# Two units of the expert modulation moved ahead of the conv branch's sums of squares, and one weight load moved behind the gate chunk's loads

## The chip, the cores and the metric

The kernel runs on one core of a Trainium2 chip. The metric is the device time of one execution in microseconds (us). Engine names are those of the profile: PE is TensorE (PEld its weight loads), DVE is VectorE, ACT is ScalarE, POOL is GpSimd, SP is SyncE, which issues the loads of all large weights.

## The reference

A trunk of two layers works on 256 tokens of width 1024. Each layer is modulated by six vectors that come from the conditioning vector `c`, and has a mixer (conv heads beside attention heads) and a mixture of 16 experts:

```python
for l in range(DEPTH):
    mod = (c_act @ w_ada[l] + b_ada[l])[:, None, :]
    shift1, scale1, gate1, shift2, scale2, gate2 = jnp.split(mod, 6, axis=-1)
    h = rmsnorm(x, norm1_g[l]) * (1.0 + scale1) + shift1
    u = h @ w_in[l]
    u_b, u_c, u_h, u_q, u_k, u_v = jnp.split(u, split_at, axis=-1)
    y_conv = short_conv_mixer(u_b, u_c, u_h, conv_w[l])
    ...
    y_att = moba_attention(q, k, v).transpose(0, 2, 1, 3).reshape(B, S, aw)
    y_mix = jnp.concatenate(
        [rmsnorm(y_conv, conv_out_g[l]), rmsnorm(y_att, attn_out_g[l])], axis=-1)
    x = x + gate1 * (y_mix @ w_out[l])
    h2 = rmsnorm(x, norm2_g[l]) * (1.0 + scale2) + shift2
    x = x + gate2 * hier_moe(h2, ...)
```

## The kernel before

All code is written by hand for each engine: an engine runs its instructions in the order in which the program lists them, and semaphores tie the engines together.

**Units and the ring.** All weights come to SBUF in units of 1 MB, into a ring of ten slots (`raw`, `RAW = 10`). The list `stream` gives the order in which SP loads them. Before a load SP waits until the unit that held the slot, ten places earlier in `stream`, is used up (`wait_free`). SP works in order, so a wait for one slot holds back all loads behind it. The kinds of unit that matter here:

- `("w", l, u)`, u = 0 to 11: the input projection `w_in`, called w0 to w11 below. The units of u = 10 and 11 hold the columns of the values `v`; u = 12 to 15 (w12 to w15) hold `w_out`. ACT copies each half of such a unit to `whi` (L500), DVE subtracts to get the low part `wlo` (L790), and PE multiplies both in three passes. A w unit is used up when DVE has made its second half (`lo_done`).
- `("a", chunk, k)`: unit k of a modulation chunk, the product of `c` with columns of `w_ada`. The chunk `G` (units G0 to G7) gives the two gates, `M` (M0 to M7) gives shift and scale of the expert sub-layer, and in layer 0 `A` (A0 to A7) gives those of the next layer's mixer. PE multiplies them in `ada_acc` (L1248, eight rows of the profile to a unit) straight from `raw`, all into PSUM bank 6, and a unit is used up when PE has done so (`ada_used`).
- `("g", ...)` and `("d", ...)`: gate, up and down weights of the experts, multiplied by PE from `raw` (L1559 and L1585).

**The mixer on PE, in order** (line numbers of the profile): the input projection of q, k and two conv parts (`in_half`, L1347 and L1354); units G0 to G3; the transposes of q and k (L1383); G4 to G7; scores of the first heads (L1397); the projection of the third conv part (halves 16 to 19, L1347) with the transposes of probabilities between (L1405); more scores; the projection of the values (halves 20 to 23, L1354); four matmuls with a matrix of ones that sum the squares of the conv output over channels (L1449); the products with the values (L1415 to L1417); M0 to M7 (L1248); the output projection (`out_half`, L1462).

**Around the sums of squares.** DVE makes the conv output (L1003 to L1007), ACT squares it (L640) and signals `csq_ready`, and PE waits for that signal ahead of L1449. ACT then takes a root (L644), and DVE scales the conv output and splits it (to L1021, `ymc_ready`), for which `out_half` waits.

**Around the units G.** DVE waits for the last unit G to add a bias (`gate_row`, L886) and then takes the maxima of the scores (L970, L975), ACT the exponentials (L590). Behind these ACT and DVE split w11 (halves 22 and 23), which the projection of the values needs.

Of the kernel before, what the change touches and what calls it, by code (L numbers as in the profile page):

```python
# [30 lines left out]
def trunk(nc, x, c, positions, norm1_g, norm2_g, w_ada, b_ada, w_in, conv_w, q_norm_g, k_norm_g,  # L31
          conv_out_g, attn_out_g, w_out, w_rg, b_rg, w_re, b_re, w_gate, w_up, w_down, out):
    _, S, D = x.shape
    L = norm1_g.shape[0]
    CW = conv_out_g.shape[1]
    AW = attn_out_g.shape[1]
    HD = q_norm_g.shape[1]
    H = AW // HD
    NE, _, F = w_gate.shape[1:]
    NG = w_rg.shape[2]  # L40
    EG = NE // NG
# [21 lines left out]
    with ExitStack() as ctx:  # L63
# [218 lines left out]
        stream = [("a", 0, k) for k in range(4)] + [("w", 0, 0), ("w", 0, 1)]  # L282
        stream += [("a", 1, 0), ("a", 1, 1), ("w", 0, 2), ("a", 1, 2), ("a", 1, 3)]
        for l in range(L):
            stream += [("w", l, u) for u in range(3 if l == 0 else 2, 12)]
            stream += [("a", chunk_of[("G", l)], k) for k in range(KD)]
            stream += [("w", l, u) for u in range(12, 16)]
            stream += [("a", chunk_of[("M", l)], k) for k in range(KD)]
            if l + 1 < L:
                stream += [("a", chunk_of[("A", l + 1)], k) for k in range(KD)]  # L290
            for p in range(NP + 1):
                if p < NP:
                    stream += [("g", l, (2 * p + i, h)) for h in range(2) for i in range(2)]
                if p > 0:
                    stream += [("d", l, 2 * (p - 1) + i) for i in range(2)]
            if l + 1 < L:
                stream += [("w", l + 1, u) for u in range(2)]
            stream.append(("x", l, 0))
# [935 lines left out]
        def _(pe):  # L1234
            def ada_acc(kind, l, ks):

                q = chunk_of[(kind, l)]
                if ks[0] == 0 and q > 0:
                    pe.wait_ge(mod_evac, steps_before[q])
                    before_q = sum(1 for name, _ in chunks[:q] if name == "G")  # L1240
                    if before_q:
                        pe.wait_ge(gate_row_ready, before_q)
                for k in ks:
                    unit = ("a", q, k)
                    pe.wait_ge(raw_full[ring_slot[unit]], landed[unit])
                    for i in range(4):
                        row = 2 * k + i // 2 if q < 2 else k
                        ins = pe.matmul(ps[32 * i:32 * i + 32, 6, :], c_rep[:, row, :],  # L1248
                                        raw[:, ring_slot[unit], i * 512:(i + 1) * 512],
                                        start=(k == 0), stop=(k == chunk_units[q] - 1), skip_group_check=True)  # L1250
                    ins.then_inc(ada_used, 1)
# [51 lines left out]
            def wait_half(l, i):  # L1303
                n = HALVES * l + i
                pe.wait_ge(lo_done, n + 1)
                return whi[:, slot(n), :], wlo[:, slot(n), :]
# [24 lines left out]
            for l in range(L):  # L1331
# [6 lines left out]
                def in_half(n, bank, k0, by_channel):  # L1338
                    w = wait_half(l, n)
                    for kk in range(2):  # L1340
                        k = k0 + kk
                        if l == 0 and n == 4 and kk == 1:
                            ada_acc("A1", 0, range(2, 4))
                        if by_channel:
                            for j in range(KC):
                                for p, (pa, pw) in enumerate(PASSES):
                                    ins = pe.matmul(ps[:, bank + j // 2, (j % 2) * S:(j % 2 + 1) * S],  # L1347
                                                    w[pw][:, kk * 512 + j * P:kk * 512 + (j + 1) * P],
                                                    acts[pa][:, k, :], start=(k == 0 and p == 0 and j % 2 == 0),
                                                    stop=(k == KD - 1 and p == 2), skip_group_check=True)  # L1350
                        else:
                            for t in range(T):
                                for p, (pa, pw) in enumerate(PASSES):
                                    ins = pe.matmul(ps[:, bank + t, :], acts[pa][:, k, t * P:(t + 1) * P],  # L1354
                                                    w[pw][:, kk * 512:(kk + 1) * 512],
                                                    start=(k == 0 and p == 0), stop=(k == KD - 1 and p == 2))
                    ins.then_inc(unit_used, 1)
# [43 lines left out]
                def probs_T(u):  # L1401
                    pe.wait_ge(exp_done, 4 * l + u + 1)
                    for h, bank, p in heads(u):
                        for q in range(3):
                            ins = pe.transpose(ps[:, bank, q * P:(q + 1) * P], p[:, q * P:(q + 1) * P],  # L1405
                                               ident[:, :])
                    ins.then_inc(pT_done, 1)

                def values(a):
                    for h in range(4 * a, 4 * a + 4):  # L1410
                        p = work[:, h // 4, h % 4, :]
                        vs = slice(h * HD, (h + 1) * HD)
                        c0 = 2 * HD * (h % 4)
                        y0, y1 = slice(c0, c0 + HD), slice(c0 + HD, c0 + 2 * HD)
                        pe.matmul(ps[:, a, y0], p[:, 0:P], v_sb[:, 0, vs], start=True, stop=True)  # L1415
                        pe.matmul(ps[:, a, y1], p[:, P:2 * P], v_sb[:, 0, vs], start=True, stop=False)
                        ins = pe.matmul(ps[:, a, y1], p[:, 2 * P:3 * P], v_sb[:, 1, vs], start=False, stop=True)  # L1417
                    ins.then_inc(pv_done, 1)
# [25 lines left out]
                probs_T(2)  # L1444
                probs_T(3)
                in_half(23, 4, 6, False)
                pe.wait_ge(csq_ready, l + 1)
                for j in range(KC):
                    ins = pe.matmul(ps[:, 7, S:2 * S], ones[:, :], cb[:, j, :], start=(j == 0), stop=(j == KC - 1))  # L1449
# [2 lines left out]
                pe.wait_ge(proj_evac, 5 * (l + 1))  # L1452
                values(0)
                values(1)
                ada_acc("M", l, range(0, 8))

                def out_half(s, half, t, ns):
                    w = wait_half(l, 24 + 4 * s + half)
# [195 lines left out]
                with pe.If(pe.value_load(over_i[0:1, l:l + 1], min_val=0, max_val=1) > 0):  # L1654
# [10 lines left out]
                    for e in range(NE):  # L1665
                        loads = X_LOADS * l + 16 * 5 * e
                        for half in range(2):
                            pe.wait_ge(x_full, loads + 32 * (half + 1))
                            w = stage.rearrange("p (g k f) -> p g k f", g=2, k=4)
# [51 lines left out]
```

## Time and profile before

| | before |
|---|---|
| median of 3 runs | 581.92 us (581.85 to 581.98) |
| profiled execution | 583.74 us |
| its span, first to last instruction | 581.8 us |
| mean granted TensorE clock | 0.978 |
| PE busy | 548.2 us, 94% |
| DVE busy | 278.4 us, 48% |
| ACT busy | 224.3 us, 39% |
| memory read | 188.12 MB, 325 GB/s over the span |

The span is what the views of the trace show; 1.94 us of the profiled execution lie around it. Busy shares are means over stages with different limits.

### The profile page before, as it was taken

How to read it: one execution, taken by the hardware profiler on the slowest of the kernel's cores; microseconds unless marked ns; L12 is line 12 of the kernel's file. 1: busy time of each engine (PE TensorE's matmuls, PEld its weight loads, DVE VectorE, ACT ScalarE, POOL GpSimd, SP SyncE). 2: the span in 40 equal slices, each digit the busy share in tenths (PEclk: the TensorE clock that was granted, in tenths of full speed). 3: DMA queues.
4: the chain of work that ended last, by engine and by line, in shares of the span. 5: the costliest groups of instructions: out<-in, count | busy, mean ns of one | idle time of the engine just before them, and what ended most of it. 6: DMA issues, size and time to landing. Idle time of an engine off the chain costs nothing.

```text
span 581.8 us, 8006 instructions
## 1 busy us (share of the span) xinstructions
PE 548.2 (94%) x3222; PEld 356.2 (61%) x3222; DVE 278.4 (48%) x475; ACT 224.3 (39%) x386; POOL 17.0 (3%) x74
## 2 busy tenths in 40 slices
PE   7899989999999999999978999999996999999996
PEld 6578939868666344443357897786674744444433
DVE  3629954993481022222358489479438202222243
ACT  2527445632346222221237264554314623222121
POOL 3105000000000000000000000000000000000000
PEclk9999999999989999999979999999997999999999
DMA  8999993972999999999997743499288379999961
GB/s 303 386 386 367 402 353 144 424 309 96 425 408 412 413 414 413 414 413 411 403 387 282 277 151 126 190 402 393 74 315 335 137 296 394 413 413 413 412 269 75
DMA packets 51759, 189.79 MB, mean 326 GB/s; under 512 B 4650, under 2 KB 4730, under 8 KB 44292
## 3 DMA queue, kind: packets, MB, share of 16 engines
q1 hardware_dynamic: 50496, 185.62, 81.8%
q0 software_dynamic: 896, 2.45, 1.2%
q10 hardware_dynamic: 324, 1.13, 0.6%
q8 instruction: 29, 0.48, 0.3%
q14 instruction: 14, 0.11, 0.1%
HBM read 188.12 MB, written 1.06 MB: 325 GB/s over the span
## 4 chain that ended last, share of the span: by engine, by line
PE 69%; DVE 17%; DMA 6%; ACT 3%; issue 2%; SPq 1%; DVEq 0%; ACTq 0%
PE ps L1559 18%; PE ps L1585 9%; PE ps L1462 7%; PE ps L1539 6%; PE ps L1354 6%; PE ps L1347 6%; DVE wlo L790 5%; PE ps L1248 5%; PE ps L1601 4%; DMA raw<-in_w_ada_dram 4%; DMA raw<-in_w_down_dram 2%; DVE work L952 2%; DVE cbc L1005 1%; DVE tokmaj L947 1%; SPq L325 1%
## 5 line engine op out<-in xcount | busy, mean ns | idle before, releaser
L790 DVE TENSOR_TENSOR wlo<-raw,whi 128x1024 fp32r<-128x1024 f32 x64 | 75.6, 1220 | 35.6 <-ACT whi L500 35.4
L500 ACT ACTIVATE whi<-raw 128x1024 fp32r<-128x1024 f32 x64 | 65.4, 1057 | 36.5 <-PE ps L1347 14.3
L1559 PE MATMUL ps<-raw,qkT 128*64 128x512 f32 x256 | 58.3, 597 | 1.6 <-ACT work L740 1.6
L1585 PE MATMUL ps<-raw,work 128*64 128x512 f32 x256 | 58.5, 598 | 1.1 <-DMA raw<-in_w_down_dram 1.1
L1559 PE MATMUL ps<-raw,cbc 128*64 128x512 f32 x256 | 57.6, 594 | 0.0
L1185 DVE SCALAR_TENSOR_TENSOR work<-ps,cw,work 128x256 f32<-128x256 f32 x16 | 10.9, 683 | 95.8 <-ACT work L734 95.8
L1171 DVE TENSOR_TENSOR v_sb<-ps,gates 128x512 f32<-128x512 f32 x32 | 22.1, 692 | 69.1 <-PE ps L1585 69.1
L1347 PE MATMUL ps<-act_hi,whi 128*128 128x256 f32 x192 | 54.9, 286 | 0.0
L1347 PE MATMUL ps<-act_hi,wlo 128*128 128x256 f32 x192 | 54.3, 283 | 0.0
L1347 PE MATMUL ps<-act_lo,whi 128*128 128x256 f32 x192 | 54.3, 283 | 0.0
L1248 PE MATMUL ps<-raw,c_rep 128*32 128x512 f32 x384 | 45.6, 605 | 4.0 <-DMA raw<-in_w_ada_dram 4.0
L722 ACT ACTIVATE whi<-v_sb 128x512 fp32r<-128x512 f32 x32 | 20.2, 630 | 58.0 <-DVE v_sb L1171 58.0
L1559 PEld LDWEIGHTS ps<-raw,cbc 128*64 128x64 f32 x256 | 18.5, 137 | 34.3 <-issue 33.2
L1354 PE MATMUL ps<-whi,act_hi 128*128 128x512 f32 x96 | 38.1, 397 | 1.3 <-DVE act_lo L893 1.3
L1347 PEld LDWEIGHTS ps<-act_hi,whi 128*128 128x128 f32 x192 | 36.8, 192 | 2.5 <-issue 2.3
L1539 PEld LDWEIGHTS ps<-whi,act_hi 128*128 128x128 f32 x128 | 26.7, 209 | 18.2 <-issue 18.2
L1539 PE MATMUL ps<-whi,act_hi 128*128 128x256 f32 x128 | 37.4, 321 | 0.3 <-DVE whi L1122 0.3
L1559 PEld LDWEIGHTS ps<-raw,qkT 128*64 128x64 f32 x256 | 17.3, 137 | 33.1 <-issue 28.0
L1354 PE MATMUL ps<-wlo,act_hi 128*128 128x512 f32 x96 | 37.4, 390 | 0.0
L1354 PE MATMUL ps<-whi,act_lo 128*128 128x512 f32 x96 | 37.4, 389 | 0.0
L1585 PEld LDWEIGHTS ps<-raw,work 128*64 128x64 f32 x256 | 17.4, 136 | 32.5 <-issue 31.7
L1347 PEld LDWEIGHTS ps<-act_hi,wlo 128*128 128x128 f32 x192 | 36.8, 192 | 0.1
(239 smaller groups left out, 862.7 us busy)
## 6 DMA issues: line engine op xcount, KB each, us to landing
raw<-in_w_ada_dram SPq DMA_DIRECT2D x40, 1024.0 KB, 12.7
raw<-in_w_gate_dram SPq DMA_DIRECT2D x64, 512.0 KB, 8.3
raw<-in_w_up_dram SPq DMA_DIRECT2D x64, 512.0 KB, 9.8
raw<-in_w_down_dram SPq DMA_DIRECT2D x32, 1024.0 KB, 11.3
raw<-in_w_in_dram SPq DMA_DIRECT2D x23, 1024.0 KB, 14.3
raw<-in_w_ada_dram SPq DMA_DIRECT2D x16, 512.0 KB, 11.4
raw<-in_w_out_dram SPq DMA_DIRECT2D x8, 1024.0 KB, 7.0
gates<-gate_line POOLq DMA_DIRECT2D x2, 1024.0 KB, 5.1
```

The lines of the kernel that those rows point to most:

```text
L500: act.activation(whi[:, slot(n), :], raw[:, r, (i % 2) * 1024:(i % 2 + 1) * 1024], ACT.Copy).then_inc(hi_done, 1)
L722: act.activation(y_hi[:, cols], y_f[:, cols], ACT.Copy).then_inc(yhi_ready, 1)
L790: dve.tensor_tensor(wlo[:, slot(n), :], raw[:, ring_slot[("w", l, i // 2)], (i % 2) * 1024:(i % 2 + 1) * 1024], whi[:, slot(n), :].bitcast ...
L1171: dve.tensor_tensor(y_f[:, cols], ps[:, 2 + n, :], gates[:, 1, cols], ALU.mult).then_inc(yg_ready, 1)
L1248: ins = pe.matmul(ps[32 * i:32 * i + 32, 6, :], c_rep[:, row, :], raw[:, ring_slot[unit], i * 512:(i + 1) * 512], start=(k == 0), stop=(k ...
L1347: ins = pe.matmul(ps[:, bank + j // 2, (j % 2) * S:(j % 2 + 1) * S], w[pw][:, kk * 512 + j * P:kk * 512 + (j + 1) * P], acts[pa][:, k, :], ...
L1354: ins = pe.matmul(ps[:, bank + t, :], acts[pa][:, k, t * P:(t + 1) * P], w[pw][:, kk * 512:(kk + 1) * 512], start=(k == 0 and p == 0), sto ...
L1462: ins = pe.matmul(ps[:, 2 * t + n, :], acts[pa][:, k, t * P:(t + 1) * P], w[pw][:, n * 512:(n + 1) * 512], start=(k == 0 and p == 0), stop ...
L1539: ins = pe.matmul(ps[:, bank, j * S:(j + 1) * S], xn[part][:, t, k * P:(k + 1) * P], sel[:, t, 256 * q:256 * (q + 1)], start=(t == 0 and p ...
L1559: ins = pe.matmul(ps[i * SLOTS:(i + 1) * SLOTS, 0, :], hg[p // 2 % 2][:, k, c0:c0 + SLOTS], ws[i][:, :, kk, :], start=(k == 0), stop=(k == ...
L1585: ins = pe.matmul(ps[i * SLOTS:(i + 1) * SLOTS, 2 + n, :], hidT[:, p % 2, kk, i * SLOTS:(i + 1) * SLOTS], ws[i][:, c0:c0 + 512], start=(kk ...
L1601: ins = pe.matmul(ps[:, 4 + 2 * t + n, :], selT[:, 2 * p + t, :], ys[part][:, n * 512:(n + 1) * 512], start=(p == 0 and part == 0), stop=( ...
```

## The change

Two edits, each in both layers. In `stream`, w11 is loaded behind the eight units of G and not ahead of them. In PE's program, units M0 and M1 are multiplied ahead of the wait for `csq_ready`, and M2 to M7 stay where the whole chunk stood.

```diff
         for l in range(L):
-            stream += [("w", l, u) for u in range(3 if l == 0 else 2, 12)]
+            stream += [("w", l, u) for u in range(3 if l == 0 else 2, 11)]
             stream += [("a", chunk_of[("G", l)], k) for k in range(KD)]
-            stream += [("w", l, u) for u in range(12, 16)]
+            stream += [("w", l, u) for u in range(11, 16)]
             stream += [("a", chunk_of[("M", l)], k) for k in range(KD)]
...
                 in_half(23, 4, 6, False)
+                ada_acc("M", l, range(0, 2))
                 pe.wait_ge(csq_ready, l + 1)
                 for j in range(KC):
                     ins = pe.matmul(ps[:, 7, S:2 * S], ones[:, :], cb[:, j, :], start=(j == 0), stop=(j == KC - 1))
...
                 values(0)
                 values(1)
-                ada_acc("M", l, range(0, 8))
+                ada_acc("M", l, range(2, 8))
```

On SP, at the end of the input projection's loads in layer 0 (`in_w_in` are w units up to w11, `in_w_ada` of 128x2x1024 the units G, `in_w_out` w12 to w15, `in_w_ada` of 128x2048 the units M and A):

```order
 L325 DMA raw<-in_w_ada_dram 128x2x512 x4
-L339 DMA raw<-in_w_in_dram 128x4x512 x9
+L339 DMA raw<-in_w_in_dram 128x4x512 x8
 L334 DMA raw<-in_w_ada_dram 128x2x1024 x8
+L339 DMA raw<-in_w_in_dram 128x4x512
 L344 DMA raw<-in_w_out_dram 128x2x1024 x4
 L334 DMA raw<-in_w_ada_dram 128x2048 x16
```

One load, w11, has moved from ahead of the eight loads of G to behind them; all others keep their order. Since the ring goes round by place in the list, the units G now take the slots that were their predecessors' (G7 the slot that w8 held, where it was w9's), w11 takes the slot of w9, and from w12 on every unit has its old slot. In some of these slots the holder has changed: w13, w14 and w15 now follow G0, G1 and G2 (before: w11, G0 and G1), M0 to M4 follow G3 to G7 (before: G2 to G6), and M5 follows w11 (before: G7).

On PE, at the end of the projection of the values in layer 0 (the last two matmuls of `in_half(23)`, then the sums of squares and the first products with the values; a row of 32x512 is a matmul of a unit of M, four to a unit):

```order
 L1354 MATMUL ps<-wlo,act_hi 128x512
 L1354 MATMUL ps<-whi,act_lo 128x512
-L1449 MATMUL ps<-cbc,ones 128x256 x4
+L1248 MATMUL ps<-raw,c_rep 32x512 x8
+L1450 MATMUL ps<-cbc,ones 128x256 x4
 L1415 MATMUL ps<-v_sb,work 128x64
 L1416 MATMUL ps<-v_sb,work 128x64
```

Eight matmuls, the units M0 and M1, now stand between the projection of the values and the sums of squares; behind the products with the values 24 of the 32 matmuls of the chunk are left. The line added moves the numbers behind it up by one.

## Rows read from the trace of the kernel before

**Rows 1.** The page: busy time of PE; GB/s in 40 slices of 14.5 us.
```profile
PE 548.2 (94%) x3222; PEld 356.2 (61%) x3222; DVE 278.4 (48%) x475; ACT 224.3 (39%) x386; POOL 17.0 (3%) x74
GB/s 303 386 386 367 402 353 144 424 309 96 425 408 412 413 414 413 414 413 411 403 387 282 277 151 126 190 402 393 74 315 335 137 296 394 413 413 413 412 269 75
```

**Rows 2.** Chain of waits, layer 0's mixer: start us, us, what.
```profile
78.13 6.80 DMA raw<-in_w_ada_dram
...
115.32 1.24 DVE cbc L1007
116.58 1.06 ACT cbc L640
```

**Rows 3.** Timeline of PE, layer 0: start us, us, instructions, [idle before <-releaser].
```profile
79.55 1.92 PE L1248 MATMUL ps<-raw,c_rep 128*32 128x512 f32 x16
82.46 1.07 PE L1248 MATMUL ps<-raw,c_rep 128*32 128x512 f32 x8 [0.98 <-DMA raw<-in_w_ada_dram]
84.98 1.79 PE L1248 MATMUL ps<-raw,c_rep 128*32 128x512 f32 x8 [1.46 <-DMA raw<-in_w_ada_dram]
86.70 2.57 PE L1397 MATMUL ps<-qkT 64*128 64x128 f32 x16
89.20 0.38 PE L1347 MATMUL ps<-act_hi,whi 128*128 128x256 f32 x1
...
117.69 1.99 PE L1449 MATMUL ps<-cbc,ones 128*128 128x256 f32 x8 [1.37 <-ACT cbc L640]
...
124.92 7.07 PE L1248 MATMUL ps<-raw,c_rep 128*32 128x512 f32 x64
131.92 0.73 PE L1462 MATMUL ps<-whi,act_hi 128*128 128x512 f32 x2
```

**Rows 4.** Timeline of PE, layer 1, the same places.
```profile
362.56 2.78 PE L1248 MATMUL ps<-raw,c_rep 128*32 128x512 f32 x24
366.00 1.06 PE L1248 MATMUL ps<-raw,c_rep 128*32 128x512 f32 x8 [0.66 <-DMA raw<-in_w_ada_dram]
367.00 1.69 PE L1397 MATMUL ps<-qkT 64*128 64x128 f32 x16
368.62 0.38 PE L1347 MATMUL ps<-act_hi,whi 128*128 128x256 f32 x1
...
397.10 1.99 PE L1449 MATMUL ps<-cbc,ones 128*128 128x256 f32 x8 [1.36 <-ACT cbc L640]
```

**Rows 5.** Windows, 84 to 90 us: after busy times, granted clock, DMA share, GB/s.
```profile
84.00:85.00 1.00, 0.02 (x3) 0.02 (x4) 0.00 (x0) 0.00 (x0) 0.00 (x0) 1.00 1.01 410
85.00:86.00 1.00, 1.00 (x8) 0.14 (x8) 0.00 (x0) 0.00 (x0) 0.00 (x0) 0.59 0.52 209
87.00:88.00 1.00, 1.00 (x8) 0.92 (x7) 0.51 (x1) 0.00 (x0) 0.20 (x1) 0.50 0.00 0
89.00:90.00 1.00, 1.00 (x9) 0.81 (x7) 0.96 (x3) 0.00 (x0) 0.23 (x1) 1.00 0.01 0
```

**Rows 6.** Timeline of SP, layer 0: loads of G6, G7, w12 and w13 to w15.
```profile
70.74 0.37 SPq L334 DMA_DIRECT2D raw<-in_w_ada_dram  x1
78.13 0.37 SPq L334 DMA_DIRECT2D raw<-in_w_ada_dram  x1
80.40 0.37 SPq L344 DMA_DIRECT2D raw<-in_w_out_dram  x1
97.66 1.39 SPq L344 DMA_DIRECT2D raw<-in_w_out_dram  x3
```

**Rows 7.** DMA issues from 70 to 71 us (G6): KB each, median us to landing.
```profile
raw<-in_w_ada_dram SPq DMA_DIRECT2D x1, 1024.0 KB, 11.7
```

**Rows 8.** Timeline of ACT, layer 0: the copies of w11's two halves.
```profile
94.14 2.23 ACT L500 ACTIVATE whi<-raw 128x1024 fp32r<-128x1024 f32 x2
```

**Rows 9.** Timeline of DVE, layer 0: the conv output's low part (`ymc_ready`).
```profile
124.66 1.23 DVE L1021 TENSOR_TENSOR act_lo<-cbc,act_hi 128x1024 fp32r<-128x1024 f32 x1
```

**Rows 10.** Timeline of PE, layer 0's expert stage: its one wait for a load.
```profile
280.86 1.51 PE L1585 MATMUL ps<-raw,work 128*64 128x512 f32 x6 [1.12 <-DMA raw<-in_w_down_dram]
```

## The prediction

> **What bounds the kernel now.** I read the page first: PE is busy for 548.2 of 581.8 us [rows 1], so time is won only where PE itself waits, or runs slowly. Then the chain of waits, in order of time, for the places where it leaves PE. In layer 0's mixer it does so twice near the edits: it goes through a load that SP issued at 78.13 and that took 6.80 us to land, and through DVE and ACT at 115.32 to 117.64 [rows 2]. PE's timeline gives the size of these holes: 0.98 us ahead of unit G6 and 1.46 us ahead of G7, both for a load, and 1.37 us ahead of the sums of squares, for ACT's squares [rows 3]. In layer 1 they are 0.66 and 1.36 us [rows 4]. A third cost shows when the two layers are laid side by side. From the start of G7 to the start of the scores PE takes 1.72 us in layer 0 (84.98 to 86.70) and 1.00 us in layer 1 (366.00 to 367.00); the scores take 2.50 us (86.70 to 89.20) against 1.62 us (367.00 to 368.62) [rows 3, 4]. The windows say why: behind the stretch in which PE stood still for 2.44 us, the granted clock drops to 0.59 and 0.50 and is back at 1.00 only when the scores are over [rows 5]; 0.50 is the lower of the two levels, 1.2 GHz, and 1.00 the upper, 2.4 GHz.
>
> **The loads of G.** G7 waits for the slot of w9, so SP issues it at 78.13, when DVE has split w9; G6, in the slot of w8, goes at 70.74 [rows 6]. G6 lands 11.7 us after its issue [rows 7], at 82.4, when PE starts on it; G7 lands at 84.93 [rows 2]. So G6 was behind other loads (one unit lands each 2.5 us), and G7 behind G6. With w11 taken out ahead of them each unit G gets the issue time, the slot and the place in the queue of the unit ahead of it: G7 is issued at 70.74 and lands at 82.4, G6 lands a unit earlier, near 79.9, and w11 takes what was G7's, issue at 78.13 and landing at 84.93.
>
> PE runs a unit in 0.875 us (7.00 us from 124.92 to 131.92 for eight [rows 3]). From 79.55 it does G4, G5 and G6 until 82.18, waits some 0.3 us, and starts G7 at 82.46 where it started at 84.98: 2.52 us. With the hole down to 0.3 us I take the clock to stay up, so that G7 and the scores cost what they cost in layer 1: 1.72 − 1.00 = 0.72 and 2.50 − 1.62 = 0.88 us. Layer 0 gains 2.52 + 0.72 + 0.88 = 4.12 us here. If the clock falls all the same, 2.52.
>
> In layer 1 G7 gets an issue time one unit earlier in the same way, and the hole of 0.66 us goes; the clock was up there already.
>
> What follows must come earlier too. DVE's maxima and ACT's exponentials hang on G7 and the scores and move with them; the projection behind them uses w8 to w10, which are split by 80.4, when SP could issue w12 into w10's slot [rows 6]. The next in line is **w11**: ACT copies it right behind the exponentials, at 94.14 [rows 8], in the new order near 90.0. It lands at 84.93, 5.1 us ahead. That is the cover that makes moving it free; each us beyond it would hold ACT, with the probabilities' copies queued behind it, for which PE's next scores wait.
>
> SP has less to wait for behind w12. Today w13 waits for w11's slot until 97.66, and w14, w15 and the first six of M stand behind it [rows 6]. Now w13 takes the slot of G0, long multiplied, so w13 to w15 and M0 to M4 follow w12 as fast as SP issues and G4 to G7 are used. At 2.5 us a unit, nine units behind w11 are there by 84.93 + 9 × 2.5 = 107.4. The bus was idle in that time: 144 GB/s in the slice from 87.3 to 101.8 [rows 1].
>
> **M0 and M1 ahead of the sums of squares.** In the trace's own times PE is free at 117.69 − 1.37 = 116.32. Two units take 1.75 us, until 118.07, so the squares, ready at 117.64, wait 0.4 us, and the chunk behind the values is 1.75 us shorter. Net the hole of 1.37 us is filled, 1.36 in layer 1. By the above M0 and M1 are there before 107. What the split chunk costs extra the trace does not show: two more changes between kinds of matmul. The nearest row is G7 ahead of the scores in layer 1, 1.00 us against 0.875, so 0.1 us; bounds 0 and 0.3 per layer. I take 0.1. The 0.4 us by which the sums end later go to ACT's root and DVE's split, which ends at 125.89 [rows 9] where the output projection starts at 131.92 [rows 3]: 6.0 us of room, of which the shorter chunk eats 1.3 and the delay 0.4.
>
> **Behind the mixer.** The output projection, the routing and the experts follow PE. The loads of the A chunk and the experts wait in SP for w14, w15 and the units M and A, the last of them paced by PE's output projection, so they come earlier along with it. I count the gain of the mixer in full.
>
> **Sum.** Layer 0: 4.12 + 1.37 − 0.1 = 5.4. Layer 1: 0.66 + 1.36 − 0.1 = 1.9. Together 7.3 us. The profiled span of 581.8 us becomes 574.5; its execution of 583.74 lies 1.82 above the median, so I take the gain off the median: 581.92 − 7.3 = **574.6 us**.
>
> **Rivals.**
> *The clock falls anyway* (PE's hole ahead of G7 does not quite close, or its time in G is too thin). Layer 0 loses 0.72 + 0.88: gain 5.7, 576.2 us. For it: at the routing and between layers PE has low stretches too, and a shift of some us may lengthen or shorten them, by a like amount. Against: eight units of M in a row run at 0.875 each, as G4 and G5 do.
>
> *M0 and M1 buy nothing*, because something else holds the output projection, such as the conv branch's split or the attention norm: 581.92 − 4.12 − 0.66 = 577.1 us. Against it are the 6.0 us of room.
>
> *The expert stage is bound by its loads.* For it: 408 to 414 GB/s through layer 0's experts, without a dip [rows 1]. If the stream of loads starts no earlier, layer 0's 5.4 us come back as waits of PE: 581.92 − 1.9 = 580.0 us. Against: in that stage PE waits for a load once, 1.12 us [rows 10], and what releases the loads moves. The Trainium skill speaks for this rival: its page "DMA: Bandwidth & Descriptors", section Specifications, puts the ceiling of the path into SBUF at 435 GB/s; the row's 413 is 95% of that, so by the page loads that start late could hardly catch up.
>
> *Slower: w11 comes late.* If the loads in flight shared the bandwidth instead of landing in order of issue, w11 would land with the nine behind it, at 107.4, and ACT, due at 90.0, would stand for 17.4 us: layer 0 ends 12.0 us later than now, 581.92 − 1.9 + 12.0 = 592 us. It decides from a landing at 90.0 + 7.3 = 97.3 on. Against: G7, with w12 issued 2.27 us behind it, landed 2.5 us after G6, one unit's time. The same page, section "Queues, rings and completion order", warns that "completion is **not FIFO per issuing engine**"; by it w11 could lose its place, by the row it does not, and I go by the row.
>
> *The edits do nothing*: the holes close but what comes next was as late, 581.9.
>
> **How the numbers follow.** The full gain: 0.58, own range 573.5 to 575.7. The clock falls: 0.15. M0 and M1 buy nothing: 0.08. Loads bind the experts: 0.06. Slower by w11: 0.05. Nothing: 0.04. A larger gain, through less time at the low clock later on, 571 to 573.4: 0.04. From 572.5 to 578.5 stand the first three and part of the larger gain, 0.83. The unknown switch cost (0 to 0.6 in sum) is inside. A measurement here tells 0.2% (1.2 us) from no change: faster 0.91, same 0.04, slower 0.05.
>
> **What would show it.** In the new trace: G7 starts without a hole of more than 0.5 us in both layers; the scores of layer 0 start 3.2 us earlier (near 83.5) at a clock of 1.00; ACT's copies of w11 start right behind the exponentials with no wait for a load; w13 to w15 are issued near 81, not 97.66; the hole ahead of L1450 is gone in both layers and the output projection of layer 0 starts near 126.5, that of layer 1 7.3 us earlier than now; PE's waits for loads among the experts stay near 1 us. I am wrong if w11 holds ACT, if the clock still dips near 85, or if waits for expert weights grow by what the mixer gave.

## The result and the profile after

The changed kernel took 579.18 us (median of 8 executions, 577.28 to 581.14), the kernel before 583.04 us (8 executions, 581.85 to 587.24): a ratio of 0.9937 with a 95% interval of 0.9916 to 0.9958. It is faster by 0.4 to 0.8%, 3.7 us by the ratio and 3.9 by the medians where 7.3 were forecast, and the 579.18 us lie above the range given. The three executions on which the forecast was based were also quick ones: the median of before rose from 581.92 to 583.04 with five more.

The profiled execution took 577.56 us. The page of the changed kernel:

```profile
span 575.8 us, 8006 instructions
...
PE 548.0 (95%) x3222; PEld 356.4 (62%) x3222; DVE 278.4 (48%) x475; ACT 224.4 (39%) x386; POOL 17.0 (3%) x74
...
PEclk9899999999989999999979999999995999999999
...
GB/s 304 388 387 368 406 382 418 373 126 155 420 408 413 413 414 414 412 415 414 397 386 291 257 147 130 414 422 131 103 381 246 147 310 408 405 415 413 412 265 76
```

The seventh slice now moves 418 GB/s where it moved 144 [rows 1]: w13 to w15 and the first units M are loaded there. PEclk, the granted clock in tenths, has an 8 in the second slice and a 5 in the 31st (432 to 446 us), where the page of before has a 9 and a 7.

PE's timeline of the changed kernel, at the places of [rows 3, 4, 10] (start, us, instructions, idle before):

```profile
15.86 1.94 PE L1248 MATMUL ps<-raw,c_rep 128*32 128x512 f32 x8 [1.17 <-DMA raw<-in_w_ada_dram]
...
80.37 3.64 PE L1248 MATMUL ps<-raw,c_rep 128*32 128x512 f32 x32
83.94 1.68 PE L1397 MATMUL ps<-qkT 64*128 64x128 f32 x16
85.56 0.39 PE L1347 MATMUL ps<-act_hi,whi 128*128 128x256 f32 x1
...
112.62 1.92 PE L1248 MATMUL ps<-raw,c_rep 128*32 128x512 f32 x16
114.47 1.99 PE L1450 MATMUL ps<-cbc,ones 128*128 128x256 f32 x8
...
121.70 5.36 PE L1248 MATMUL ps<-raw,c_rep 128*32 128x512 f32 x48
126.99 0.73 PE L1463 MATMUL ps<-whi,act_hi 128*128 128x512 f32 x2
...
275.85 1.51 PE L1586 MATMUL ps<-raw,work 128*64 128x512 f32 x6 [1.05 <-DMA raw<-in_w_down_dram]
...
357.54 3.64 PE L1248 MATMUL ps<-raw,c_rep 128*32 128x512 f32 x32
361.12 1.68 PE L1397 MATMUL ps<-qkT 64*128 64x128 f32 x16
...
389.79 1.92 PE L1248 MATMUL ps<-raw,c_rep 128*32 128x512 f32 x16
391.65 1.99 PE L1450 MATMUL ps<-cbc,ones 128*128 128x256 f32 x8
...
404.16 0.74 PE L1463 MATMUL ps<-whi,act_hi 128*128 128x512 f32 x2
```

Every hole that the change aimed at is gone: G4 to G7 are one run of 32 rows, and M0 and M1 lead straight into the sums of squares, in both layers. The output projection starts 4.93 us earlier in layer 0 (131.92 to 126.99) and 7.18 us earlier in layer 1 (411.34 to 404.16). At the end of the span 6.0 us are left.

SP's loads of G7, w11, w12 to w15 and M0 to M3 in the changed kernel, where [rows 6] stand for before, and ACT's copies of w11 as in [rows 8]:

```profile
71.57 0.37 SPq L334 DMA_DIRECT2D raw<-in_w_ada_dram  x1
78.96 0.37 SPq L339 DMA_DIRECT2D raw<-in_w_in_dram  x1
81.23 1.91 SPq L344 DMA_DIRECT2D raw<-in_w_out_dram  x4
83.18 1.93 SPq L334 DMA_DIRECT2D raw<-in_w_ada_dram  x4
```

```profile
90.65 2.08 ACT L500 ACTIVATE whi<-raw 128x1024 fp32r<-128x1024 f32 x2
```

w13 to w15 go out near 82 instead of 97.66, and ACT finds w11 there: the row shows no wait.

Two sets of windows of the changed kernel, at G7 and the scores and in the routing of layer 1 (granted clock third from the end):

```profile
84.00:86.00 2.00, 2.00 (x21) 1.62 (x20) 1.73 (x3) 0.00 (x0) 0.57 (x1) 1.00 1.02 406
...
432.00:434.00 2.00, 1.29 (x6) 1.29 (x7) 1.15 (x3) 1.19 (x2) 0.00 (x0) 0.50 1.02 406
...
446.00:448.00 2.00, 2.00 (x11) 2.00 (x11) 0.65 (x5) 1.31 (x3) 0.00 (x0) 0.50 0.03 8
```

The low clock of [rows 5] is gone. In the routing of layer 1 the clock is at its lower level from 431.8 to 448.9, 17.1 us, where it was low from 440.2 to 443.6 and from 447.0 to 453.8 in the trace of before, 10.2 us; PE has the same waits for ACT and DVE in both. Windows of before:

```profile
442.00:444.00 2.00, 1.79 (x16) 0.48 (x12) 1.72 (x3) 1.84 (x4) 0.00 (x0) 0.60 1.07 434
444.00:446.00 2.00, 0.59 (x4) 0.52 (x4) 1.80 (x5) 0.22 (x1) 0.00 (x0) 1.00 0.99 410
450.00:452.00 2.00, 2.00 (x11) 2.00 (x11) 1.90 (x8) 0.30 (x1) 0.00 (x0) 0.50 0.00 0
```

The early stretch at 15.4 to 18.8 us is outside the change: PE had waited 1.17 us for one of the first loads.

### The profile page after: what moved, and what is told of

Read it like the earlier page. It is cut to its first block, busy times and chain, and to the rows that moved or that the text cites. A ratio compares the mean times of both kernels' runs of the same rounds, so it can differ in the third digit from the quotient of the medians.

```text
span 575.8 us, 8006 instructions
## 1 busy us (share of the span) xinstructions
PE 548.0 (95%) x3222; PEld 356.4 (62%) x3222; DVE 278.4 (48%) x475; ACT 224.4 (39%) x386; POOL 17.0 (3%) x74
## 4 chain that ended last, share of the span: by engine, by line
PE 87%; DMA 4%; DVE 4%; ACT 3%; issue 1%; SPq 1%; DVEq 0%; ACTq 0%
PE ps L1560 18%; PE ps L1347 12%; PE ps L1354 12%; PE ps L1586 9%; PE ps L1248 7%; PE ps L1463 7%; PE ps L1540 6%; PE ps L1602 4%; DMA raw<-in_w_down_dram 2%; DMA raw<-in_w_ada_dram 2%; PE ps L1397 1%; PE ps L1405 1%; PE ps L1296 1%; PE ps L1271 1%; PE ps L1450 1%
```

## The experiments

Two theories were set against each other at first. C: the gain is there in every execution, and the low clock elsewhere takes part of it back. S: the trace of before was not typical, and the gain was sized too large from it.

**The same two kernels again.** No edit.

again_after: 

> The changed kernel once more. Theory C (clock): the mixers give about 7 us in every execution, and what the time lacks is lost at the low granted clock elsewhere (start, routing, start of layer 1), by other amounts in each execution. It expects the output projection of layer 1 about 7 us earlier than in the kernel before, counted from the start of layer 0's first projection, and a ratio of 0.990 to 0.996. Theory S (size): part of the holes that the change closes was not there in most executions of the kernel before, so the mixers give only 4 us in a typical execution; a second trace then shows again 7 us for this kernel, but a second trace of the kernel before shows smaller holes.

again_before: 

> The kernel before once more, for a second trace. Theory C: the holes ahead of units G6 and G7 (0.98 and 1.46 us) and ahead of the sums of squares (1.37 us) are there again, the low clock at 85 to 89 us too; the low-clock stretches at the routing differ in number. Theory S: the holes ahead of G6 and G7 come to under 1 us in sum, or the clock stays up there. Ratio 0.998 to 1.002 by both.

Measured: the changed kernel 579.10 us (12 executions), ratio 0.9927 (0.9900 to 0.9954); the kernel before 583.79 against 582.81 (12 and 35 executions), 1.0014 (0.9993 to 1.0034). The second trace of the kernel before differs from the first just where the forecast was sized. PE's timeline there:

```profile
80.19 2.78 PE L1248 MATMUL ps<-raw,c_rep 128*32 128x512 f32 x24
84.46 1.06 PE L1248 MATMUL ps<-raw,c_rep 128*32 128x512 f32 x8 [1.49 <-DMA raw<-in_w_ada_dram]
85.46 1.68 PE L1397 MATMUL ps<-qkT 64*128 64x128 f32 x16
```

and the windows behind the hole:

```profile
85.00:86.00 1.00, 1.00 (x14) 0.53 (x8) 0.40 (x1) 0.00 (x0) 0.00 (x0) 1.00 0.54 209
87.00:88.00 1.00, 1.00 (x9) 0.93 (x8) 0.96 (x3) 0.00 (x0) 0.15 (x1) 1.00 0.10 29
```

PE starts the first projection 0.7 us later (24.7 against 24.0) while the loads are no later, so there is no hole ahead of G6, one of 1.49 us ahead of G7, and the clock stays up. Theory S holds for layer 0. Counted from layer 0's first projection, layer 1's output projection does come 7.0 us earlier in again_after than in again_before, as theory C expected, but only 5.0 of them come from the mixers; the other 2.0 lie behind mixer 0, where again_before waits for a load of the experts (below).

**Each edit alone.** The two hunks of the diff, one at a time.

stream_only: 

> Only the first edit: w11 loaded behind the units G. By the sum of the prediction: layer 0 gains 4.1 us by the start of the third conv part's projection, layer 1 0.7 us; the holes ahead of the sums of squares stay at 1.37 us. Theory C: the trace shows these gains, the time 4.8 us less, give or take 2 us of low clock elsewhere (ratio 0.988 to 0.996). Theory S: the trace shows them, the time gains 2 us or less (ratio 0.996 to 1.000).

m_only: 

> Only the second edit: M0 and M1 multiplied ahead of the sums of squares. By the prediction: the holes of 1.37 us there go in both layers, less 0.1 each for the switch, and the holes ahead of G6 and G7 stay with the low clock behind them. Theory C: 2.5 us less, give or take 2 us (ratio 0.992 to 0.999). Theory S: about 2.5 us less as well, since this hole depends on no load (ratio 0.995 to 0.997).

Measured (12 executions each): stream_only 580.44, ratio 0.9962 (0.9940 to 0.9983); m_only 581.93, 0.9987 (0.9966 to 1.0008). Each edit closes its own holes in its trace and no other; in m_only the hole ahead of G7 is 1.50 us and the clock stays up behind it too. By the ratios the times are 2.2 and 0.8 us better, with intervals too wide to tell the second from nothing. For m_only both theories expected about 2.5 us, which lies outside its interval. Its mixers are shorter than those of again_before by 0.9 and 1.5 us, but in the routing of layer 1 its trace has 13.7 us of low clock (438.6 to 452.4), where again_before has 6.8.

The traces also show where layer 0's expert stage differs between executions. In stream_only PE waits there for the same down unit as in [rows 10], but longer, and the clock falls behind the wait:

```profile
277.29 4.92 PE L1585 MATMUL ps<-raw,work 128*64 128x512 f32 x14 [2.52 <-DMA raw<-in_w_down_dram]
```

```profile
276.00:278.00 2.00, 0.71 (x4) 0.40 (x6) 0.00 (x0) 0.00 (x0) 0.00 (x0) 1.00 1.05 430
278.00:280.00 2.00, 2.00 (x8) 0.72 (x6) 0.00 (x0) 0.00 (x0) 0.00 (x0) 0.57 0.97 402
```

A wait of 2.4 to 2.5 us with a low clock behind it stands in again_before and m_only as well; in these three the gather ahead of the experts ran at full clock (4.0 us from its start to that of the first gate matmuls). In the first trace of before and in both traces of the changed kernel the clock was low at the gather (5.5 us), PE came to the experts 1.5 us later, and the wait is 1.0 to 1.1 us. What one place loses the other gains: the stage waits for its loads either way. That made a third theory, L: layer 0's expert stage waits for its loads, and turns an earlier start of PE into a longer wait.

**Filling the routing's waits, and loading the last expert pair in the order of use.** The first adds matmuls whose result nobody reads; the second moves two loads.

```diff
                     ada_acc("A", l + 1, range(0, 4))
+                else:
+                    spin(6, 6)
...
+                spin(6, 2) if l + 1 == L else spin_7(2)
                 pe.wait_ge(rows_ready, l + 1)
...
+                    spin_7(2)
+                else:
+                    spin(6, 10)
                 pe.wait_ge(asg_ready, l + 1)
```

```diff
+                last = p == NP - 1
                 if p < NP:
-                    stream += [("g", l, (2 * p + i, h)) for h in range(2) for i in range(2)]
+                    stream += [("g", l, (2 * p + i, h)) for h in range(1 if last else 2) for i in range(2)]
                 if p > 0:
                     stream += [("d", l, 2 * (p - 1) + i) for i in range(2)]
+                if last:
+                    stream += [("g", l, (2 * p + i, 1)) for i in range(2)]
```

(Four more filling matmuls stand between the two groups of transposes in layer 1.)

before_fill: 

> The kernel before, with matmuls of the identity with ones (result unused) in the waits of the routing, 22 in layer 1 (bank 6, free there) and 4 in layer 0 (upper half of bank 7), so that TensorE hardly stands still there. Theory C (the clock at the routing): no stretch of low clock from 435 to 456 us and none near 170; some 1 to 2.5 us less than the kernel before, unless the loads of the experts take it back. Theory L (loads): layer 0's expert stage waits for a weight of the down projection near 278 us for 2 to 2.5 us and the clock falls there, so that what layer 0's routing gains is lost again, and only layer 1's part is left, about 1 us.

after_fill: 

> The changed kernel with the same matmuls in the waits of the routing. Theory C: the low stretch of 17 us at the routing of layer 1 (431 to 449) is gone, and the kernel is 5.1 us faster than the kernel before with the same matmuls (the mixers of two traces: 102.1 against 105.1 in layer 0, 97.1 against 99.2 in layer 1), against 4.0 without them. A rival, that the early units M cost something of their own behind the mixer (slower products, a later release of loads), expects 4.0 or less here too.

after_dfirst: 

> The changed kernel, and in the expert stage the last pair's upper halves of gate and up are loaded behind the two down units of the pair ahead, not ahead of them, as PE uses them. Theory L (the expert stage of layer 0 waits for its loads and turns earlier starts into waits): the wait for a down unit near 275 us (1.0 us in two traces, 2.5 us with a low clock behind it in three others) goes, 1 to 4 us less than the changed kernel. If the stage is bound by the loads' bandwidth throughout, the wait only moves to the units loaded later, and the time stays within 0.5 us of the changed kernel.

after_dfirst_fill: 

> Both additions on the changed kernel. If theories C and L hold, the two gains add up: 573 to 576 us where the kernel before takes 582.8, ratio 0.984 to 0.989, and less spread between executions. If the loads bind the whole stage, no faster than the changed kernel with the filling matmuls alone.

| kernel | us | ratio to before (95% interval) | executions |
|---|---|---|---|
| before_fill | 581.50 | 0.9978 (0.9960 to 0.9995) | 12 |
| after_fill | 577.37 | 0.9911 (0.9890 to 0.9933) | 6 |
| after_dfirst | 574.81 | 0.9868 (0.9843 to 0.9893) | 6 |
| after_dfirst_fill | 570.01 | 0.9800 (0.9773 to 0.9827) | 5 |

The filling shortens the low clock in the routing of layer 1 to 3.4 us in both traces, but the distance between the kernels, 4.1 us, is what it was without it (3.7 and 4.2), not the 5.1 that theory C expected. So theory C alone is not the account of what lacks. after_fill also shows theory L: with no low clock at layer 0's gather, PE waits 2.43 us for the down unit and the clock falls from 275.8 to 279.3. before_fill waits there too, 2.80 us, but its clock stays up behind the wait; and in layer 1's experts after_fill waits 1.50 us for a down unit where before_fill waits 0.44. In these two traces the changed kernel so loses 1.7 us behind mixer 0 and 0.7 behind mixer 1. The reordered loads remove these waits, as PE's timeline of after_dfirst shows at the place in layer 0:

```profile
271.20 3.60 PE L1563 MATMUL ps<-raw,cbc 128*64 128x512 f32 x16
274.64 3.60 PE L1589 MATMUL ps<-raw,work 128*64 128x512 f32 x16
278.07 3.60 PE L1563 MATMUL ps<-raw,cbc 128*64 128x512 f32 x16
```

and the stage is not bound by bandwidth there, only by the order of four loads. The kernel gains 4.3 us, a little more than the 1 to 4 expected, and more than the wait of 1.0 us that its two earlier traces show at this place. The trace also has less low clock in the routing of layer 1 (6.8 us against 17.1); whether that comes from the four loads is not shown. With both additions 570.01 us were measured, below the 573 to 576 expected, and 571.27 for the same kernel again (after_quiet below): 7.8 to 9.1 us less than the changed kernel, where the two additions give 1.7 and 4.3 us singly. Why they more than add up is open.

**The change again, on the quiet kernel, and the hole ahead of G7 filled.** The first three kernels carry both additions, with neither edit, both, or the second alone. The last is the kernel before with:

```diff
-                ada_acc("G", l, range(4, 8))
+                ada_acc("G", l, range(4, 6))
+                spin_7(4 if l == 0 else 0)
+                ada_acc("G", l, range(6, 7))
+                spin_7(6 if l == 0 else 0)
+                ada_acc("G", l, range(7, 8))
```

before_quiet: 

> The kernel before with the later-loaded halves of the last expert pair and the filling matmuls in the routing, that is, the best version less the change of this study. If the change gives what the mixers of the traces say (about 3 us in layer 0, 2 us in layer 1) and the rest was lost to the experts' loads and to the low clock at the routing, this kernel is 4.9 us slower than the version with the change: 574 to 576 us. If the change is worth only the 4 us seen without these additions, or the change and the reordered loads gain the same microseconds, 573 to 574 us.

after_quiet: 

> The best version once more (the changed kernel, the last pair's loads in the order of use, filling matmuls in the routing), for a second trace on the chip of the kernel without the change: 569.5 to 571 us, ratio 0.978 to 0.982; mixers again 102.2 and 97.2 us.

m_quiet: 

> Only the second edit (M0 and M1 early), on the kernel with both additions. The mixers of the trace say 0.9 to 1.3 us in each layer: 2.2 to 2.6 us less than the version without the change. If the early units M cost something behind the mixer, as the 0.9 us measured without the additions may mean, 1 us or less.

hole_fill: 

> The kernel before, with ten matmuls of the identity with ones (result unused) in the holes ahead of G6 and G7 of layer 0, so that TensorE hardly stands still there and its clock can't fall behind them; the loads stay as they were. The prediction counted 1.6 us for the low clock behind these holes. If it falls there in most executions, 1 to 1.6 us less than the kernel before; if only in some, as in one of the three traces of kernels that have this hole unchanged, 0.5 us or less.

| kernel | us | ratio to before (95% interval) | executions |
|---|---|---|---|
| before_quiet | 578.04 | 0.9917 (0.9891 to 0.9943) | 6 |
| after_quiet | 571.27 | 0.9801 (0.9778 to 0.9824) | 5 |
| m_quiet | 573.20 | 0.9848 (0.9822 to 0.9873) | 5 |
| hole_fill | 583.79 | 1.0014 (0.9999 to 1.0030) | 12 |

hole_fill bears on the clock at 85 us. The clock stays at 1.00 there, and the kernel is not faster: 583.79 us against 582.76, from 0.1 us faster to 1.7 slower by the interval. But the filling has a price. In its trace G7 is issued at 78.41 and lands 6.1 us later, at 84.5, and PE, still filling, starts on it 0.8 us after that:

```profile
83.79 1.60 PE L1282 MATMUL ps<-ones,ident 128*128 128x128 f32 x12
85.33 1.06 PE L1248 MATMUL ps<-raw,c_rep 128*32 128x512 f32 x8
86.32 1.68 PE L1402 MATMUL ps<-qkT 64*128 64x128 f32 x16
```

If it costs 0.8 us in the other executions as well, the clock's part is 0.9 us at most, so the 1.6 us were not in a typical execution of the kernel before.

before_quiet missed its expectation by some 2 us on the slow side: with the additions the change is worth 6.8 us, not 4.9 (ratio of the two ratios 0.9883; with the two half-widths of 0.0023 and 0.0026 added in squares, 0.985 to 0.992, or 4.7 to 8.8 us). after_quiet lies 0.3 us above its expectation (569.5 to 571). m_quiet is faster than before_quiet by 4.8 us (medians) or 4.0 (ratios; 1.9 to 6.1, worked out in the same way), where 2.2 to 2.6 were expected. So the second edit, worth 0.8 us alone on the kernel before, costs nothing of its own behind the mixer in this kernel.

The lengths of the stages, from the starts on PE in each trace. A mixer runs from the first projection's start to that of the output projection; what is behind it runs to the next layer's first projection, or in layer 1 to the start of the last run of L1602 (its number in the kernel after):

| trace | mixer 0 | behind 0 | mixer 1 | behind 1 |
|---|---|---|---|---|
| before (first) | 107.9 | 180.1 | 99.3 | 161.9 |
| again_before | 105.1 | 182.2 | 99.2 | 163.3 |
| before_fill | 105.9 | 180.2 | 99.1 | 161.4 |
| before_quiet | 104.5 | 177.2 | 99.3 | 160.9 |
| hole_fill | 106.4 | 180.0 | 99.2 | 162.2 |
| stream_only | 103.5 | 182.0 | 98.4 | 162.3 |
| m_only | 104.2 | 181.6 | 97.8 | 162.6 |
| m_quiet | 103.3 | 176.1 | 97.8 | 159.2 |
| after (first) | 102.1 | 180.1 | 97.1 | 163.0 |
| again_after | 102.2 | 180.2 | 97.2 | 163.1 |
| after_fill | 102.2 | 181.9 | 97.1 | 162.1 |
| after_dfirst | 102.2 | 178.4 | 97.3 | 161.4 |
| after_dfirst_fill | 102.2 | 177.2 | 97.2 | 160.7 |
| after_quiet | 102.2 | 176.3 | 97.1 | 159.5 |

The mixers of the changed kernel are the same to 0.2 us in six traces. Those of the kernel before are not: mixer 0 takes 104.5 to 105.9 us in three traces (106.4 in hole_fill, with the price of its filling) and 107.9 in the one from which the forecast was made. The change is worth 105.2 (the mean of the three) − 102.2 = 3.0 us in layer 0, and 99.2 − 97.1 = 2.1 in layer 1.

## Why the prediction was wrong

**The step that failed** is the term "Layer 0 gains 2.52 + 0.72 + 0.88 = 4.12 us here". It was worked out rightly for the execution at hand, whose own pair of traces even gives more: mixer 0 went from 107.9 to 102.1. But that execution was not typical. PE started its first projection 0.7 to 1.2 us earlier than in the five other traces of kernels that keep the holes (again_before, before_fill, before_quiet, m_only, m_quiet), while it could start G7 at much the same time (84.98 against 84.15 to 85.51), so the holes were larger. And its clock fell behind them, where it stayed up in all five. In again_before and m_only only the hole ahead of G7 is as large. before_fill has both holes, a smaller one ahead of G6, and its scores take 1.68 us at full clock:

```profile
82.98 1.07 PE L1248 MATMUL ps<-raw,c_rep 128*32 128x512 f32 x8 [0.60 <-DMA raw<-in_w_ada_dram]
85.51 1.07 PE L1248 MATMUL ps<-raw,c_rep 128*32 128x512 f32 x8 [1.47 <-DMA raw<-in_w_ada_dram]
86.51 1.68 PE L1404 MATMUL ps<-qkT 64*128 64x128 f32 x16
```

Counted from the first projection, the scores start after 60.8 us on the mean of these five (60.1 to 61.6) and after 59.1 in the changed kernel: the term is worth 1.7 us, not 4.12. The rival "the clock falls anyway" looked for the risk on the wrong side: in the kernel after the clock does stay up; it had mostly stayed up before as well. So the sum, put right, is 1.7 + 1.3 in layer 0 (from the scores to the output projection PE takes 44.34 us in again_before and 43.05 in the changed kernel) and 2.1 in layer 1, 5.1 us.

**The mechanism** was right at each step. G7 takes the issue time of G6, the holes ahead of it close in both layers, w11 is there before ACT wants it, w13 to w15 go out 15 us earlier, and the hole ahead of the sums of squares is filled; M0 and M1 cost 1.85 us there (112.62 to 114.47) where the chunk behind got shorter by 1.7 (7.0 to 5.29 us). Layer 1 gained 2.1 where 1.9 were forecast. "M0 and M1 buy nothing" and "Slower: w11 comes late" fall with the traces.

**"I count the gain of the mixer in full"** is open to about 1 us. The rest of 5.1 − 3.7 to 4.2 stands behind the mixers, where single traces differ by up to 2 us for the same kernel: in the first two traces of the changed kernel the routing of layer 1 had 17 us of low clock, in the first of before 10.2 and in the second 6.8. The mean granted clock on record for every execution points the same way over many executions: its median is 0.972 and 0.973 in the two sets of the changed kernel (8 and 12 executions) and 0.978 for the kernel before (35). With both additions it is the other way round, 0.990 in after_quiet against 0.9875 in before_quiet. Yet filling the routing alone did not widen the distance, though it brought the two close (0.985 in after_fill, 0.988 in before_fill); with the experts' loads reordered as well it came to 6.8 us. The intervals of the two, 2.3 to 5.5 us (worked out as above) and 4.7 to 8.8, both hold 5.1. The traces are not the medians either: the two profiled executions of the changed kernel lie 1.6 and 1.1 us below theirs, those of the kernel before 0.7 and 1.3 above, so that the pairs of traces differ by 6.2 and 7.0 us. That the waits and falls behind the mixers took back 1 us in the kernel as it stands, and gave 1 to 2 in the quiet one, is argued and not shown; why early units M should go with a longer low clock in the routing is open.

**The rival "The expert stage is bound by its loads"** was half right. The loads move along with PE (SP issues the first expert units at 141.31, 5.2 us earlier than 146.48), and no 5 us came back. But the 1.12 us of [rows 10], quoted against it, were small only because the clock was low at the gather of that execution; with the gather at full clock the wait is 2.4 to 2.8 us in six traces. It is a wait on the order of loads: four units put in the order of their use end it. The ceiling that the page "DMA: Bandwidth & Descriptors" of the Trainium skill gives (section Specifications) was not what held PE at that place, since the stream ran at much the same rate, 407 to 416 GB/s in the slices of after_dfirst, without the wait.

**The base** was off as well: 581.92 us from three executions, 583.04 from eight and 582.6 to 582.8 from later sets. That is 1.1 of the 4.6 us between 574.6 and 579.18; the gain, 7.3 against 3.9, is the other 3.4.

## What to carry to other kernels

A stage priced from one trace inherits that execution's luck: price a hole by what sets its two ends (here the landing of a load, and PE's own progress), and count a low clock behind it only if more than one trace shows it. Where loads come through a ring in one order, moving one unit changes who follows whom in the slots, also for units behind its new place (here w13 to w15); list that before and after. After closing holes, look for the wait downstream that was short only because PE came late, and put loads in the order in which they are used.

## What the hardware showed beyond that

The granted clock falls at places that differ between executions of the same kernel. Behind the hole ahead of G7 it fell in one trace (1.46 us, with 0.98 ahead of G6) and stayed at 1.00 in three (1.49 in again_before, 1.50 in m_only, 1.47 in before_fill with 0.60 ahead of G6). Behind the wait for the down unit in layer 0 it fell in again_before, m_only, stream_only and after_fill (2.41 to 2.53 us), and stayed up in before_fill (2.80) and hole_fill (2.47). What a fall costs shows in layer 0's scores, 2.50 us at the lower level against 1.62 at the upper. Executions of the kernel before spread from 580.4 to 586.9 us among 35; the changed kernel with both additions, whose PE has fewer waits, spread from 569.7 to 572.8 among ten in two sets.
